# Two decoder blocks on one core: the first block's FFN up-projection with 512-column products and a PSUM bank per output tile

## The chip, the cores and the metric

The kernel runs on one core of a Trainium2 chip. It is one launch: weights and inputs come from device memory, a 256x1024 result goes back. The metric is the device time of that core in microseconds (us). TensorE is PE below, VectorE is DVE, ScalarE is ACT, GpSimdE is POOL.

## What is computed

Two blocks with two layers each. Every layer ends with an FFN. The FFN of the first block is the part that the change touches. With 256 tokens, model width 1024 and hidden width 2816:

```python
def causal_dwconv(x, w):              # K = 3 taps along the tokens
    y = xp[:, 0:S] * w[0]
    for j in range(1, K):
        y = y + xp[:, j:j + S] * w[j]

def conv_ffn(xn, w_up, conv_w, w_down):
    h = causal_dwconv(xn @ w_up, conv_w)      # 1024 -> 5632
    g, u = jnp.split(h, 2, axis=-1)
    return (jax.nn.silu(g) * u) @ w_down      # 2816 -> 1024

# first block, layer in (0, 1):
h = h + conv_ffn(rmsnorm(h, norm_ffn[layer]), ffn_w_up[layer], ffn_conv[layer], ffn_w_down[layer])
# second block: the same without the convolution
x = x + ((jax.nn.silu(a) * b) @ w_ffn_out[i])
```

## The kernel before

All large products are computed in three parts. A weight w and an activation x are each split into a high part (rounded to the fp32r format) and a low part (the remainder), and the product is w_hi·x_hi + w_hi·x_lo + w_lo·x_hi, accumulated in PSUM.

**Units and pieces.** Weights arrive as units of 1024x512 in a ring of two slots. A unit of the up-projection, `{L}up{j}` with j = 0 to 10, holds 256 gate columns and 256 up columns, so four output tiles of 128 channels x 256 tokens: tiles 0 and 1 are gate, 2 and 3 are up. A unit is eight pieces of 128x512. For each piece ACT writes `w_hi` (a copy that rounds, `round_weights`), POOL writes `w_lo` (ring minus `w_hi`, `remainders`), and PE multiplies. `w_hi` and `w_lo` have four places (HELD = 4). ACT may round piece p once PE has started piece p−3 (semaphore `piece_started`).

**PE in an up unit.** In block 1 (`split_channel_major`, lines 755 to 786) a piece is four times two products of 256 columns with `w_hi` (lines 774 and 777) and then four of 256 columns with `w_lo` (line 781). Two tiles share a 512-column bank; a unit uses two of banks 0 to 3. In block 2 the units up1 to up10 are WIDE (`split_wide`): x_hi and x_lo lie side by side in `x_pair`, so a piece is four products of 512 columns with `w_hi` (line 796) and four of 256 with `w_lo` (line 801). Each tile then has a bank of its own, with w_hi·x_lo in its second half.

**ACT and DVE in block 1 (`ffn_conv`, one on each engine).** For each pair q of tiles (q = 0 gate, q = 1 up), DVE multiplies the bank by the rows' norm factor R_b (`scale_bank`, line 2419, semaphore `ff_scaled`); ACT writes the last tap of the convolution into SBUF, two activations (`last_tap`, `ff_in`); DVE adds the two earlier taps with four instructions (`earlier_taps`, line 2456). After q = 0 a tiny copy on DVE (line 2461, `ff_conv`) releases ACT's SiLU (line 1845), which writes bank 4 or 5. DVE waits for it (`ff_act`), forms the product in bank 6 or 7 (line 2473), rounds it into `f_hi` and subtracts for `f_lo` (lines 2437 and 2439).

**Order.** Each engine follows its own program strictly in the written order; nothing is scheduled at run time. ACT, for unit j of block 1 with j > 0: last_tap(j,0), round pieces 0 and 1 of unit j+1, SiLU(j), round 2 and 3, last_tap(j,1), round 4 to 7. For j = 10 the following unit is down0, and only piece 2 is rounded between SiLU and last_tap(10,1). In layer 1 ACT also issues DMAs after the rounding (`load_block2`). DVE: scale(j,0), taps(j,0), scale(j,1), taps(j,1), product, split. The down projection follows with pieces of 128x512 rows; its piece 0 takes two banks (2 and 3), its piece 4 the other two (0 and 1).

Of the kernel before, what the change touches and what calls it, by code (L numbers as in the profile page):

```python
# [25 lines left out]
ALU = mybir.AluOpType  # L26
ACT = mybir.ActivationFunctionType
# [3 lines left out]
SEQ = 256  # L31
# [174 lines left out]
def build(nc, I, consts, out):  # L206

    ctx = ExitStack()
    with ctx:
# [203 lines left out]
        xs_ready = sem("xs_ready")  # L413
        ff_scaled = sem("ff_scaled")
        vec_ready = sem("vec_ready")
        zero_ready = sem("zero_ready")
# [134 lines left out]
        SPLIT = BY_CHANNELS | BY_TOKENS | BY_ROWS  # L551
        WIDE = {f"{L}up{j}" for L in (2, 3) for j in range(1, FF_UNITS)}
        AFTER_NORM = {"eq", "odq"} | {f"{L}up0" for L in range(4)} | {"2qr0", "3qr0"}
# [80 lines left out]
        def gains(key):  # L634

            L = int(key[0])
            if key == "2m":
                return lambda k: g_both[:, k:k + 1]
            name = {"m": "norm_mix", "x": "norm_xattn", "f": "norm_ffn"}[key[1]] + ("_g_2" if L >= 2 else "")
            r0 = ROWS[name][0] + 8 * (L % 2)  # L640
            return lambda k: vecs[:, r0 + k:r0 + k + 1]

        def turned_bank(key, k):
# [1005 lines left out]
        def _(act):  # L1649
# [175 lines left out]
            def ffn_conv(L):  # L1825
                first_unit(f"{L}up0", f"{L}f")
                r0 = ROWS["ffn_conv"][0] + L * 3 * 2 * FF_TILES + 2 * 2 * FF_TILES

                def last_tap(j, q):

                    n = L * FF_UNITS + j
                    key = (f"{L}up{j}", q)
                    b = B.uses[key][0]
                    act.wait_ge(ff_scaled, 2 * n + q + 1)
                    if q == 0 and n >= 2:
                        act.wait_ge(ff_h, n - 1)
                    for c in range(2):
                        row = r0 + q * FF_TILES + 2 * j + c
                        m = copy(f_y[j % 2][:, 2 * q + c, :], bank[b][:, c * SEQ:(c + 1) * SEQ], scale=vecs[:, row:row + 1])
# [292 lines left out]
        def _(dve):  # L2132
# [281 lines left out]
            def scale_bank(key):  # L2414
# [18 lines left out]

            def split_hidden(v, hi, lo, j):

                drain()
                nc.vector.tensor_copy(hi[:, 2 * j:2 * j + 2, :], v)
                drain()
                tt(lo[:, 2 * j:2 * j + 2, :], v, hi[:, 2 * j:2 * j + 2, :], ALU.subtract).then_inc(ff_h, 1)

            def ffn_conv(L):
# [4 lines left out]
                def earlier_taps(j, q):  # L2446

                    b, y = B.uses[(f"{L}up{j}", q)][0], f_y[j % 2]
                    dve.wait_ge(ff_in, 2 * (L * FF_UNITS + j) + q + 1)
                    for tap in (1, 0):  # L2450
# [3 lines left out]
                        for c in range(2):  # L2454
                            row = r0 + tap * 2 * FF_TILES + q * FF_TILES + 2 * j + c
                            m = stt(y[:, 2 * q + c, late:], bank[b][:, c * SEQ:(c + 1) * SEQ - late], vecs[:, row:row + 1],
                                    y[:, 2 * q + c, late:], ALU.mult, ALU.add)
                    m.then_inc(empty[b], 1)
                    drain()
# [3 lines left out]
                for j in range(FF_UNITS):  # L2463
                    scale_bank((f"{L}up{j}", 0))
                    if j == 0:
                        scale_bank((f"{L}up{j}", 1))
                    earlier_taps(j, 0)
                    if j:
                        scale_bank((f"{L}up{j}", 1))
                    earlier_taps(j, 1)  # L2470
                    dve.wait_ge(ff_act, L * FF_UNITS + j + 1)
                    product = bank[6 + j % 2][:, :]
                    tt(product, bank[4 + j % 2][:, :], f_y[j % 2][:, 2:4, :].rearrange("p a b -> p (a b)"), ALU.mult)
                    split_hidden(product.rearrange("p (a b) -> p a b", a=2), f_hi, f_lo, j)

# [446 lines left out]
```

## Time and profile before

| | |
|---|---|
| time, median of 3 runs | 2060.34 us (2060.13 to 2060.78) |
| the profiled execution, its own time | 2063.64 us |
| its span, first to last instruction | 2061.8 us |
| PE busy | 2014.0 us, 98% |
| POOL busy | 1624.4 us, 79% |
| ACT busy | 1088.3 us, 53% |
| DVE busy | 870.2 us, 42% |
| mean granted PE clock | 0.99 of full |

The span is what the trace covers; the time is 1.8 us more in the same execution, and the median of the unprofiled runs is 3.3 us under that. The up stage of layer 0 in block 1 lies at about 232 to 347 us of the span, that of layer 1 at about 713 to 828 us; the WIDE units of block 2 lie at about 1299 to 1411 us and 1881 to 1992 us. PE's ends are modelled, so the distance between starts of consecutive instructions says more than their durations.

### The profile page before, as it was taken

The numbers are of one execution on the slowest core, as the hardware profiler recorded it, in microseconds if no ns is written. First come the engines' busy times: TensorE is split into PE (matmuls) and PEld (weight loads), VectorE is DVE, ScalarE is ACT, GpSimd is POOL, SyncE is SP. The second block draws the span as 40 slices with busy tenths as digits, with TensorE's granted clock in tenths as the row PEclk, the third lists the DMA queues.
The fourth block names the chain that finished last, engine by engine and source line by source line (L and its number), as shares of the span: only waits on it lengthen the run. The fifth ranks groups of instructions, "written<-read, shape, count | busy, mean of one in ns | idle before, by whom it ended". The sixth has DMA issues, their size and how long they took to land.

```text
span 2061.8 us, 32417 instructions
## 1 busy us (share of the span) xinstructions
PE 2014.0 (98%) x12407; PEld 1755.8 (85%) x12407; DVE 870.2 (42%) x2029; ACT 1088.3 (53%) x2124; POOL 1624.4 (79%) x1293
## 2 busy tenths in 40 slices
PE   9999999999999999999999989999999999999998
PEld 8798999897889899898778858888997788678886
DVE  5512565065532466173323272563332412644551
ACT  4454665455244566445454585544444554865444
POOL 6595898976386798999799608899997897268998
PEclk9999999989999999999999999999999999999999
DMA  9753555543054476565446605555554466235553
GB/s 306 140 189 118 184 184 185 183 159 103 1 173 155 153 237 215 169 199 190 137 167 191 220 22 164 184 184 187 181 188 159 143 196 224 78 110 177 190 201 109
DMA packets 244271, 343.14 MB, mean 166 GB/s; under 512 B 8819, under 2 KB 172755, under 8 KB 243989
## 3 DMA queue, kind: packets, MB, share of 16 engines
q1 hardware_dynamic: 231832, 330.83, 48.7%
q10 hardware_dynamic: 12285, 10.24, 2.5%
q8 instruction: 99, 1.62, 0.3%
q14 instruction: 55, 0.45, 0.1%
HBM read 336.85 MB, written 4.19 MB: 165 GB/s over the span
## 4 chain that ended last, share of the span: by engine, by line
PE 84%; POOL 6%; DVE 3%; issue 3%; ACT 2%; POOLq 1%; DMA 1%; DVEq 0%; SPq 0%; ACTq 0%
PE bank L774 9%; PE bank L781 9%; PE bank L777 9%; PE bank L796 7%; PE bank L824 7%; PE bank L830 7%; PE bank L827 6%; POOL w_lo L1557 5%; PE bank L854 5%; PE bank L857 5%; PE bank L861 5%; PE bank L801 4%; DVE E L2271 1%; DVE E L2285 1%; PE bank L742 1%
## 5 line engine op out<-in xcount | busy, mean ns | idle before, releaser
L1557 POOL TENSOR_TENSOR w_lo<-ring,w_hi 128x512 fp32r<-128x512 f32 (+1 forms) x1216 | 1577.5, 1317 | 387.4 <-ACT w_hi L1652 351.3
L1652 ACT ACTIVATE w_hi<-ring 128x512 fp32r<-128x512 f32 (+1 forms) x1216 | 757.5, 630 | 789.2 <-PE bank L824 265.2
L774 PE MATMUL bank<-x_pair,w_hi 128*128 128x256 f32 x1504 | 380.8, 285 | 2.2 <-DVE x_pair L2171 1.5
L777 PE MATMUL bank<-x_pair,w_hi 128*128 128x256 f32 x1504 | 378.3, 284 | 0.0
L824 PE MATMUL bank<-w_hi,x_pair 128*128 128x512 f32 (+1 forms) x752 | 299.1, 398 | 2.6 <-issue 1.6
L774 PEld LDWEIGHTS bank<-x_pair,w_hi 128*128 128x128 f32 x1504 | 289.5, 192 | 5.0 <-issue 1.5
L827 PE MATMUL bank<-w_hi,x_pair 128*128 128x512 f32 (+1 forms) x752 | 292.8, 390 | 0.0
L777 PEld LDWEIGHTS bank<-x_pair,w_hi 128*128 128x128 f32 x1504 | 289.6, 193 | 0.4
L781 PE MATMUL bank<-x_pair,w_lo 128*128 128x256 f32 x1504 | 242.2, 283 | 0.0
L830 PE MATMUL bank<-w_lo,x_pair 128*128 128x512 f32 (+1 forms) x752 | 234.3, 393 | 3.4 <-POOL w_lo L1557 2.6
L781 PEld LDWEIGHTS bank<-x_pair,w_lo 128*128 128x128 f32 x1504 | 208.1, 193 | 0.0
L854 PE MATMUL bank<-w_hi,hidden 128*128 128x512 f32 x480 | 187.2, 390 | 0.0
L857 PE MATMUL bank<-w_hi,hidden 128*128 128x512 f32 x480 | 186.8, 389 | 0.0
L830 PEld LDWEIGHTS bank<-w_lo,x_pair 128*128 128x128 f32 x752 | 139.9, 190 | 41.3 <-POOL w_lo L1557 13.6
L796 PE MATMUL bank<-x_pair,w_hi 128*128 128x512 f32 x640 | 174.7, 394 | 0.0
L824 PEld LDWEIGHTS bank<-w_hi,x_pair 128*128 128x128 f32 x752 | 143.7, 191 | 33.1 <-issue 5.3
L827 PEld LDWEIGHTS bank<-w_hi,x_pair 128*128 128x128 f32 x752 | 143.7, 191 | 28.0 <-issue 0.7
L861 PE MATMUL bank<-w_lo,hidden 128*128 128x512 f32 x480 | 147.8, 389 | 0.0
L796 PEld LDWEIGHTS bank<-x_pair,w_hi 128*128 128x128 f32 x640 | 109.4, 189 | 14.7
L801 PEld LDWEIGHTS bank<-x_pair,w_lo 128*128 128x128 f32 x640 | 98.2, 189 | 13.6
L2163 DVE TENSOR_TENSOR h<-bank,h 128x512 f32<-128x512 f32 x36 | 23.1, 684 | 202.9 <-PE bank L861 153.7
L854 PEld LDWEIGHTS bank<-w_hi,hidden 128*128 128x128 f32 x480 | 90.1, 188 | 18.9 <-issue 0.4
(328 smaller groups left out, 2444.5 us busy)
## 6 DMA issues: line engine op xcount, KB each, us to landing
ring<-in_w_in SPq DMA_DIRECT2D x74, 1024.0 KB, 5.0
ring<-in_ffn_w_up SPq DMA_DIRECT2D x44, 1024.0 KB, 5.1
ring<-in_w_ffn_in SPq DMA_DIRECT2D x44, 1024.0 KB, 5.1
ring<-in_ffn_w_down SPq DMA_DIRECT2D x20, 1024.0 KB, 4.9
ring<-in_w_ffn_out SPq DMA_DIRECT2D x20, 1024.0 KB, 4.9
ring<-in_xattn_wkv SPq DMA_DIRECT2D x16, 1024.0 KB, 5.3
ring<-in_w_o_ret SPq DMA_DIRECT2D x16, 1024.0 KB, 4.9
ring<-in_od_w_in SPq DMA_DIRECT2D x12, 1024.0 KB, 5.2
```

Of the source, the lines that this page charges most:

```text
L774: m = mm(out_, view(w_hi)[:, k, :], x_hi[:, 4 * kh + k, :], start=start, stop=False)
L777: mm(out_, view(w_hi)[:, k, :], x_lo[:, 4 * kh + k, :], start=False, stop=False)
L781: m = mm(out_, view(w_lo)[:, k, :], x_hi[:, 4 * kh + k, :], start=False, stop=stop)
L796: m = mm(bank[b][:, :], view(w_hi)[:, k, :], x_pair[:, 4 * kh + k, :, :].rearrange("p a n -> p (a n)"), start=kh == 0 and k == 0, stop=False)
L824: m = mm(acc, hi, view(w_hi), start=k == 0, stop=False)
L827: mm(acc, lo, view(w_hi), start=False, stop=False)
L830: m = mm(bank[b0 + t][:, 0:n], x_hi[:, k, t * P:(t + 1) * P], view(w_lo), start=False, stop=k == KT - 1)
L854: m = mm(bank[b][:, :], hi, view(w_hi), start=kt == 0, stop=False)
L857: mm(bank[b][:, :], lo, view(w_hi), start=False, stop=False)
L861: m = mm(bank[b][:, :], x_hi[:, kt, t * P:(t + 1) * P], view(w_lo), start=False, stop=kt == tiles - 1)
L1557: tt(view(w_lo), src, view(w_hi), ALU.subtract).then_inc(w_lo_ready, 1)
L1652: return A(o, i_, ACT.Copy, **kw)
```

## The change

Units up1 to up10 of the two layers of block 1 become WIDE as well (unit up0 stays as it was). What follows from that in the code:

- PE: four 512-column products per piece in place of eight of 256 columns; a bank for each of the four tiles (0, 4, 1, 5 or 2, 6, 3, 7).
- ACT: `cross_terms(j, q)` copies the second half of two banks (w_hi·x_lo of two tiles) to the SBUF tile E, ahead of `last_tap(j, q)`.
- DVE: `scale_tiles` adds E to the first half of the bank, and multiplies by R_b, tile by tile.
- SiLU is written to the bank of the unit's first tile, and product and split happen there. A further tiny copy on DVE, after the split, releases that bank; the other three are released by the taps.

```diff
-        WIDE = {f"{L}up{j}" for L in (2, 3) for j in range(1, FF_UNITS)}
+        WIDE = {f"{L}up{j}" for L in range(4) for j in range(1, FF_UNITS)}
...
+                def cross_terms(j, q):
+
+                    if j == 0:
+                        return
+                    n = L * FF_UNITS + j
+                    if q == 0:
+                        act.wait_ge(ff_scaled, 2 * n)
+                    for c in (2 * q, 2 * q + 1):
+                        key = (f"{L}up{j}", c)
+                        B.wait_full(act, key)
+                        copy(E[:, c, 0:SEQ], bank[B.uses[key][0]][:, SEQ:2 * SEQ]).then_inc(ff_cross, 1)
...
-                    A(bank[4 + j % 2][:, :], f_y[j % 2][:, 0:2, :].rearrange("p a b -> p (a b)"), ACT.Silu).then_inc(ff_act, 1)
+                    A(bank[B.uses[f"{L}up{j}", 0][0]][:, :], f_y[j % 2][:, 0:2, :].rearrange("p a b -> p (a b)"), ACT.Silu).then_inc(ff_act, 1)
...
                     else:
+                        cross_terms(j, 0)
                         last_tap(j, 0)
                         round_weights(following, 0, 2)
                         silu(j)
                         round_weights(following, 2, HELD - 1 if j + 1 == FF_UNITS else HELD)
+                        cross_terms(j, 1)
                         last_tap(j, 1)
...
+            def scale_tiles(L, j, q):
+
+                if j == 0:
+                    return scale_bank((f"{L}up{j}", q))
+                for c in range(2):
+                    dve.wait_ge(ff_cross, 4 * (L * (FF_UNITS - 1) + j - 1) + 2 * q + c + 1)
+                    v = up_tile(L, j, q, c)
+                    tt(v, v, E[:, 2 * q + c, 0:SEQ], ALU.add)
+                drain()
+                for c in range(2):
+                    v = up_tile(L, j, q, c)
+                    m = tt(v, v, R_b[:, :], ALU.mult)
+                m.then_inc(ff_scaled, 1)
...
                 tt(lo[:, 2 * j:2 * j + 2, :], v, hi[:, 2 * j:2 * j + 2, :], ALU.subtract).then_inc(ff_h, 1)
+                drain()
+                nc.vector.tensor_copy(small[:, 22, 1:2], small[:, 23, 1:2]).then_inc(empty[b], 1)
```

Three places show what stands where. ACT in unit j = 3 of layer 0, before: two last-tap activations (`region<-bank2`), two roundings, SiLU (line 1845), two roundings, the other pair.

```order
L1652 ACTIVATE region<-bank2,vecs 128x256 [waits ff_h,ff_scaled]
L1652 ACTIVATE region<-bank2,vecs 128x256
L1652 ACTIVATE w_hi<-ring 128x512 [waits piece_started,half0_landed0]
L1652 ACTIVATE w_hi<-ring 128x512 [waits piece_started]
L1845 ACTIVATE bank6<-region 128x512 [waits ff_conv]
```

ACT in the same unit after the change, up to the roundings of pieces 4 to 7.

```order
L1660 ACTIVATE E<-bank2 128x256 [waits bank_full2,ff_scaled]
L1660 ACTIVATE E<-bank6 128x256 [waits bank_full6]
L1660 ACTIVATE region<-bank2,vecs 128x256 [waits ff_h,ff_scaled]
L1660 ACTIVATE region<-bank6,vecs 128x256
L1660 ACTIVATE w_hi<-ring 128x512 [waits piece_started,half0_landed0]
L1660 ACTIVATE w_hi<-ring 128x512 [waits piece_started]
L1863 ACTIVATE bank2<-region 128x512 [waits ff_conv]
L1660 ACTIVATE w_hi<-ring 128x512 [waits piece_started,half0_landed0]
L1660 ACTIVATE w_hi<-ring 128x512 [waits piece_started]
L1660 ACTIVATE E<-bank3 128x256 [waits bank_full3]
L1660 ACTIVATE E<-bank7 128x256 [waits bank_full7]
L1660 ACTIVATE region<-bank3,vecs 128x256 [waits ff_scaled]
```

Two copies to E stand ahead of each pair of last taps; those of the second pair (banks 3 and 7) stand behind the SiLU and two roundings.

DVE from the product of the unit before (line 2473) to the taps of this one, before.

```order
L2473 TENSOR_TENSOR bank6<-bank4,region 128x512 [waits ff_act]
L2437 CAST hidden<-bank6 128x512
L2439 TENSOR_TENSOR hidden<-bank6,hidden 128x512
L2419 TENSOR_TENSOR bank2<-bank2,R_b 128x512 [waits bank_full2]
L2456 SCALAR_TENSOR_TENSOR region<-bank2,vecs,region 128x255 [waits ff_in]
```

The same stretch of DVE after the change, and on to the second pair of tiles.

```order
L2513 TENSOR_TENSOR bank0<-bank0,region 128x512 [waits ff_act]
L2472 CAST hidden<-bank0 128x512
L2474 TENSOR_TENSOR hidden<-bank0,hidden 128x512
L2476 COPY small<-small 128x1
L2448 TENSOR_TENSOR bank2<-bank2,E 128x256 [waits ff_cross]
L2448 TENSOR_TENSOR bank6<-bank6,E 128x256 [waits ff_cross]
L2452 TENSOR_TENSOR bank2<-bank2,R_b 128x256
L2452 TENSOR_TENSOR bank6<-bank6,R_b 128x256
L2493 SCALAR_TENSOR_TENSOR region<-bank2,vecs,region 128x255 [waits ff_in]
```

One multiplication of 512 columns has become two additions and two multiplications of 256, and the additions wait for ACT's copies where the multiplication waited for PE.

PE at the fifth piece of down0 (k = 0 of its second half of columns), after the change; before, the row reads the same with line 854.

```order
L862 MATMUL bank0<-w_hi,hidden 128x512 [waits w_hi_ready,bank_empty1,bank_empty0]
L865 MATMUL bank0<-w_hi,hidden 128x512
```

What moved there is not the row but what empties bank 0: before, the taps of pair 0 of unit up10 (line 2456); now the tiny copy behind the split of that unit (line 2476).

## Rows read from the trace of the kernel before

**Rows 1.** The page: PE's busy time, share and instructions.
```profile
PE 2014.0 (98%) x12407; PEld 1755.8 (85%) x12407; DVE 870.2 (42%) x2029; ACT 1088.3 (53%) x2124; POOL 1624.4 (79%) x1293
```

**Rows 2.** Windows, busy us of each engine (instructions), clock, DMA share, GB/s.
```profile
core 0: us, PE busy (x) PEld busy (x) DVE busy (x) ACT busy (x) POOL busy (x), PEclk, DMA share, GB/s
242.50:333.50 91.00, 91.00 (x761) 91.00 (x760) 57.55 (x114) 57.66 (x104) 83.04 (x65) 1.00 0.58 186
1310.00:1411.00 101.00, 101.00 (x578) 88.25 (x578) 60.51 (x176) 50.36 (x90) 93.83 (x73) 1.00 0.57 187
```

**Rows 3.** Lines, 242 to 335 us: busy, mean ns, idle before, releaser.
```profile
L774 PE MATMUL bank<-x_pair,w_hi 128*128 128x256 f32 x259 | 65.0, 283 | 0.0
L1652 ACT ACTIVATE w_hi<-ring 128x512 fp32r<-128x512 f32 x66 | 41.6, 632 | 31.1 <-PE bank L774 30.4
```

**Rows 4.** Timeline (start, us, instruction): PE, consecutive pieces in block 1 and block 2.
```profile
269.52 0.28 PE L774 MATMUL bank<-x_pair,w_hi 128*128 128x256 f32 x1
...
270.96 0.28 PE L774 MATMUL bank<-x_pair,w_hi 128*128 128x256 f32 x1
...
1324.35 1.09 PE L796 MATMUL bank<-x_pair,w_hi 128*128 128x512 f32 x4
...
1325.75 1.09 PE L796 MATMUL bank<-x_pair,w_hi 128*128 128x512 f32 x4
```

**Rows 5.** Timeline of ACT in unit up10 of layer 0: last taps, then SiLU.
```profile
342.45 0.84 ACT L1652 ACTIVATE region<-bank,vecs 128x256 f32<-128x256 f32 x2
...
345.43 0.60 ACT L1845 ACTIVATE bank<-region 128x512 f32<-128x512 f32 x1
```

**Rows 6.** Timeline of ACT in unit up1 of layer 0.
```profile
240.56 0.84 ACT L1652 ACTIVATE region<-bank,vecs 128x256 f32<-128x256 f32 x2 [1.77 <-DVE bank L2419]
...
243.53 0.60 ACT L1845 ACTIVATE bank<-region 128x512 f32<-128x512 f32 x1 [1.09 <-DVE small L2461]
244.07 1.14 ACT L1652 ACTIVATE w_hi<-ring 128x512 fp32r<-128x512 f32 x2
245.11 0.82 ACT L1652 ACTIVATE region<-bank,vecs 128x256 f32<-128x256 f32 x2
```

**Rows 7.** ACT: block 2's SiLU of two tiles (timeline); copies to E (by lines).
```profile
1328.12 0.64 ACT L2109 ACTIVATE region<-bank 128x256 f32<-128x256 f32 x2
...
L1652 ACT ACTIVATE E<-bank 128x256 f32<-128x256 f32 x4 | 1.5, 380 | 5.4 <-PE bank L1371 5.3
```

**Rows 8.** Timeline of DVE, 256-column operations and the tiny copy in block 2.
```profile
1320.62 0.42 DVE L2427 TENSOR_TENSOR bank<-bank,R_b 128x256 f32<-128x256 f32 x1
...
1321.78 0.76 DVE L2431 TENSOR_TENSOR bank<-bank,E 128x256 f32<-128x256 f32 x2
...
1330.60 0.76 DVE L2866 TENSOR_TENSOR hidden<-bank,hidden 128x256 fp32r<-128x256 f32 x2
...
1331.52 0.41 DVE L2426 TENSOR_TENSOR E<-bank,R_b 128x256 f32<-128x256 f32 x1
```

**Rows 9.** Timeline of DVE in layer 0: taps, product, and last step of the split.
```profile
326.05 1.82 DVE L2456 SCALAR_TENSOR_TENSOR region<-bank,vecs,region 128x255 f32<-128x255 f32 x4 [0.91 <-ACT region L1652]
327.96 0.70 DVE L2473 TENSOR_TENSOR bank<-bank,region 128x512 f32<-128x512 f32 x1
...
329.50 0.69 DVE L2439 TENSOR_TENSOR hidden<-bank,hidden 128x512 fp32r<-128x512 f32 x1
```

**Rows 10.** Timeline: DVE's split of unit up0, and PE's down0 piece 4, layer 0.
```profile
239.23 0.69 DVE L2439 TENSOR_TENSOR hidden<-bank,hidden 128x512 fp32r<-128x512 f32 x1
...
352.75 0.39 PE L854 MATMUL bank<-w_hi,hidden 128*128 128x512 f32 x1
```

**Rows 11.** Timeline, layer 1: ACT at unit up1, and DVE's taps of pair 0 of up10.
```profile
719.05 2.57 ACTq L1876 DMA_DIRECT2D region<-constants  x5
721.74 0.84 ACT L1652 ACTIVATE region<-bank,vecs 128x256 f32<-128x256 f32 x2 [2.44 <-DVE bank L2419]
...
823.84 1.82 DVE L2456 SCALAR_TENSOR_TENSOR region<-bank,vecs,region 128x255 f32<-128x255 f32 x4 [0.91 <-ACT region L1652]
```

**Rows 12.** Windows, columns as in Rows 2: a stretch in which PE is idle a fifth.
```profile
550.00:560.00 10.00, 7.85 (x63) 7.28 (x64) 7.04 (x18) 1.28 (x8) 1.21 (x2) 1.00 0.00 0
```

More of the change, by code:

```diff
@@ L414, in build @@
         ff_scaled = sem("ff_scaled")
+        ff_cross = sem("ff_cross")
         vec_ready = sem("vec_ready")
@@ L641, in gains, with up_tile @@
             return lambda k: vecs[:, r0 + k:r0 + k + 1]
+        def up_tile(L, j, q, c):
+            name = f"{L}up{j}"
+            if name in WIDE:
+                return bank[B.uses[name, 2 * q + c][0]][:, 0:SEQ]
+            return bank[B.uses[name, q][0]][:, c * SEQ:(c + 1) * SEQ]
         def turned_bank(key, k):
@@ L1827, in ffn_conv @@
                 r0 = ROWS["ffn_conv"][0] + L * 3 * 2 * FF_TILES + 2 * 2 * FF_TILES
+                def cross_terms(j, q):
[8 more added lines that the diff above has]
+                        copy(E[:, c, 0:SEQ], bank[B.uses[key][0]][:, SEQ:2 * SEQ]).then_inc(ff_cross, 1)
                 def last_tap(j, q):
                     n = L * FF_UNITS + j
-                    key = (f"{L}up{j}", q)
-                    b = B.uses[key][0]
                     act.wait_ge(ff_scaled, 2 * n + q + 1)
@@ L1838, in last_tap @@
                         row = r0 + q * FF_TILES + 2 * j + c
-                        m = copy(f_y[j % 2][:, 2 * q + c, :], bank[b][:, c * SEQ:(c + 1) * SEQ], scale=vecs[:, row:row + 1])
+                        m = copy(f_y[j % 2][:, 2 * q + c, :], up_tile(L, j, q, c), scale=vecs[:, row:row + 1])
                     m.then_inc(ff_in, 1)
@@ L2432, in scale_wide, with split_hidden @@
                 m.then_inc(ff_scaled, 1)
-            def split_hidden(v, hi, lo, j):
+            def split_hidden(b, hi, lo, j):
+                v = bank[b][:, :].rearrange("p (a b) -> p a b", a=2)
                 drain()
@@ L2446, in earlier_taps @@
                 def earlier_taps(j, q):
-                    b, y = B.uses[(f"{L}up{j}", q)][0], f_y[j % 2]
+                    name, y = f"{L}up{j}", f_y[j % 2]
                     dve.wait_ge(ff_in, 2 * (L * FF_UNITS + j) + q + 1)
@@ L2455, in earlier_taps @@
                             row = r0 + tap * 2 * FF_TILES + q * FF_TILES + 2 * j + c
-                            m = stt(y[:, 2 * q + c, late:], bank[b][:, c * SEQ:(c + 1) * SEQ - late], vecs[:, row:row + 1],
+                            m = stt(y[:, 2 * q + c, late:], up_tile(L, j, q, c)[:, 0:SEQ - late], vecs[:, row:row + 1],
                                     y[:, 2 * q + c, late:], ALU.mult, ALU.add)
-                    m.then_inc(empty[b], 1)
+                            if tap == 0 and j and (q or c):
+                                m.then_inc(empty[B.uses[name, 2 * q + c][0]], 1)
+                            if tap == 0 and j == 0 and q and c:
+                                m.then_inc(empty[B.uses[name, q][0]], 1)
                     drain()
@@ L2463, in ffn_conv @@
                 for j in range(FF_UNITS):
-                    scale_bank((f"{L}up{j}", 0))
+                    scale_tiles(L, j, 0)
                     if j == 0:
-                        scale_bank((f"{L}up{j}", 1))
+                        scale_tiles(L, j, 1)
                     earlier_taps(j, 0)
                     if j:
-                        scale_bank((f"{L}up{j}", 1))
+                        scale_tiles(L, j, 1)
                     earlier_taps(j, 1)
                     dve.wait_ge(ff_act, L * FF_UNITS + j + 1)
-                    product = bank[6 + j % 2][:, :]
-                    tt(product, bank[4 + j % 2][:, :], f_y[j % 2][:, 2:4, :].rearrange("p a b -> p (a b)"), ALU.mult)
-                    split_hidden(product.rearrange("p (a b) -> p a b", a=2), f_hi, f_lo, j)
+                    b = B.uses[f"{L}up{j}", 0][0]
+                    tt(bank[b][:, :], bank[b][:, :], f_y[j % 2][:, 2:4, :].rearrange("p a b -> p (a b)"), ALU.mult)
+                    split_hidden(b, f_hi, f_lo, j)
             cross(0)
```

## The prediction

> **What bounds the kernel now.** Read the busy shares first [rows 1]: PE is busy 98% of the span, so a stage costs what PE costs in it, as long as the other engines keep up. The table by stage [rows 2] shows that in both up stages PE never pauses, while POOL works 83 of 91 us, ACT 58 and DVE 58. The groups by line [rows 3] say the same from the other side: PE's products have no idle time before them, and ACT's roundings spent 31.1 us waiting, 30.4 of it for PE. So in block 1 ACT and DVE are followers with slack, and the stage goes at PE's pace. The timeline gives that pace [rows 4]: a piece starts 1.44 us after the last one in block 1 (269.52 to 270.96) and 1.40 us in the WIDE units of block 2 (1324.35 to 1325.75). A unit of eight pieces is 11.52 us against 11.22 us.
>
> **What the change buys on PE.** 0.037 us a piece (11.22/8 against 1.44), 8 pieces, 10 units, 2 layers: 5.9 us, if PE goes on setting the pace. Rows stand for this: block 2 does the same products. The Trainium skill has a rule that speaks against even that (TensorE: Matmul & The Clock Gate, section "Wait — 56ns, not 53.3ns?"): a warm matmul starts N/2.4 GHz plus about 2.5 ns after the one before. By that page a piece would be estimated at 12 x 109 ns = 1.31 us before and 4 x 216 + 4 x 109 = 1.30 us after, a gain of 1.6 us in all. The rows differ from it, with 120 ns for each 256-column product (1.44/12), and they decide.
>
> **What the change adds.** PE needs rounded weights, and these come from ACT, which does its list in order. So the question is how long ACT and DVE need for one unit when each waits for the other. I follow one unit round the loop, from T0, the end of the two last-tap activations of pair 0, to the same point one unit later. Each step starts when the one before has ended:
>
> 1. T0 to the start of SiLU (DVE's taps of pair 0 and the tiny copy lie in between): 342.45+0.84 = 343.29 to 345.43, 2.14 us [rows 5]. The two roundings that ACT does meanwhile are hidden.
> 2. SiLU and two roundings, start of SiLU to start of the next activation: 243.53 to 245.11, 1.58 us [rows 6].
> 3. Two copies to E, which is the added wait: DVE can do nothing for pair 1 before. Plain copies of this form have a row of 380 ns for one [rows 7]; for two in a row the nearest is the SiLU of two tiles, 0.64 us. Bounds: 0.64 and 2 x 0.38 = 0.76. I take 0.64, since activations overlap in all rows of pairs, plus 0.04 to reach DVE: 0.68.
> 4. The second addition (0.42), a drain (0.07) and two multiplications (0.76) [rows 8]: 1.25. The drain is what is left between 0.70 busy and the 0.77 from step to step of product and split, half of 327.96 to 329.50 [rows 9].
> 5. ACT's two last taps of pair 1, as DVE's idle time shows it: 0.91 [rows 9].
> 6. DVE's taps of pair 1 to the start of the product: 326.05 to 327.96, 1.91.
> 7. Product and split: 327.96 to 329.50+0.69, 2.23.
> 8. The new tiny copy that frees the bank: 1330.60+0.76 to 1331.52, 0.16 [rows 8].
> 9. Two additions, drain, two multiplications for pair 0 of the next unit: 0.76+0.07+0.76 = 1.59. Their copies to E are ready by then: ACT is through with the last taps of pair 1 at T0+6.5, with four roundings of 0.52 each (244.07 to 245.11 is two) at about 8.5 and with the copies at about 9.2, against 10.9.
> 10. ACT's last taps of pair 0: 0.87 (0.91 less the way to DVE).
>
> The sum is 13.32 us. That is more than PE's 11.22 and more than the 11.52 of now, so **this loop takes over as the bound**. Before the change the loop did not close this way: DVE scaled pair 1 as soon as PE had it, without ACT. Now pair 1 waits behind SiLU and two roundings, and SiLU waits for DVE. What queues behind ACT's waits is rounding, so POOL's remainders and PE's pieces come late: PE waits some 2.1 us a unit, before pieces 0 and 4, on `w_hi`. POOL needs 8 x 1.28 (83.04/65 [rows 2]) = 10.2 us of each 13.3 and stays out of it.
>
> ACT standing still at a wait while later work is ready is in the rows: 1.09 us before SiLU at 243.53 [rows 6]. The Trainium skill states it as a rule (PSUM — Partial Sum Buffer, section "Engine vs sequencer instructions"): the ScalarE and VectorE queues are strictly first in, first out.
>
> **Layer 0.** Unit up1: DVE's split of up0 ends at 239.23+0.69 = 239.92 [rows 10]; plus steps 8 to 10 (0.16+1.59+0.87) T0 is 242.54, where it was 240.56+0.84 = 241.40 [rows 6]. Nine loops of 13.32 are 119.9, so T0 of up10 comes at 362.4 instead of 343.3 [rows 5]: +19.1. Then a second cost: piece 4 of down0 takes bank 0, which now is free only after up10's split. From T0 that is steps 1 to 7 with one rounding fewer (10.70−0.52) and about 0.2 for the copy, 10.4; before, piece 4 started at 352.75 [rows 10], 9.46 after T0. That adds 0.9 to 1.0. Behind it the down stage runs at PE's pace as before, so the loss stays: 20.1 us.
>
> **Layer 1.** ACT issues DMAs ahead of up1 until 719.05+2.57 = 721.62 and then did the last taps at 721.74 [rows 11]. Now the copies start there: 721.74+0.64+0.04+1.25+0.87 = 724.54 against 722.58, +1.96. T0 of up10: 724.54+119.9 = 844.4 against 823.8, +20.6; with the bank 21.6 us. The DMA issues of the later units (two each) fall where ACT has 1.7 us of slack.
>
> Sum 41.7 us. The profiled execution took 2063.64 (span 2061.8); the median is 3.3 lower, and I add to the median: 2060.3+41.7 = **2102.0 us**, 2.0% slower. A measurement of this kernel can tell about 0.2% (4 us) from no change.
>
> **Rivals.**
> *The clock falls.* PE would be idle 2.1 of 13.3 us, in pieces of about 1 us. Where it was idle 2.15 of 10 us, the granted clock stayed at 1.00 [rows 12], the 2.4 GHz level. If it fell to 1.2 GHz, a unit would need 22.4 us of PE, more than the loop; ten such units among the twenty would add (22.4−13.3) x 10 = 91 us at most, two of them 18: about 2120.
> *DVE alone sets the pace.* If the copies of pair 1 were always there in time, the loop would be steps 1, 9, 5, 6, 7, 8, 9 and 10: 2.14+1.59+0.91+1.91+2.23+0.16+1.59+0.87 = 11.40, near the 11.52 of now. T0 of up10 would be late by 1.8 and 3.4 us (1.14 and 1.96 at the start, and 9 x 11.40 = 102.6 against 101.9 and 101.2), less 0.4 in each layer since bank 0 is free at 9.0 and not at 9.46: 2064.6. For it: each engine alone has time enough. Against it: the written order, SiLU ahead of these copies.
> *The other side, faster.* If the loop took less than 11.22, PE's pace held and the 5.9 us came: 2054.4. It decides at 11.22: the loop would have to be 2.1 us shorter than my sum, and no single step but the first, sixth and seventh is as much as that. The page's matmul rule would make of this 2058.7.
>
> **Chances.** Forecast 0.87; clock 0.06; DVE alone 0.04; faster 0.03. Within the forecast an error of 0.35 us in the loop is 18 x 0.35 = 6.3 us, and step 3 at its upper bound adds 0.12 x 18 = 2.2; something of the steps may also overlap more than single rows show, so I go further down than up: 2090 to 2112. That leaves out the rivals (0.13) and a little of the forecast. Slower by over 0.2%: 0.87, 0.06 and half of DVE alone, 0.95; within 0.2%: 0.02; faster: 0.03.
>
> **What would show it.** Right: in a middle unit of layer 0 the taps of pair 0 start 13.3 us apart; DVE's first addition for pair 1 waits about 2.0 us for ACT's copy (step 2 and the first copy of step 3); PE idles before `w_hi` of two pieces a unit; block 2's up stages are unchanged at 11.22; down0's piece 4 waits for DVE's tiny copy. Wrong: a distance of 11.2 (PE) or 11.4 (DVE alone); a granted clock under 1.00 in the stage; additions from E much longer than 0.42, or PE waits for POOL.

## The result and the profile after

| | before | after |
|---|---|---|
| time, median of 4 runs each | 2060.24 us (2057.85 to 2060.78) | 2108.18 us (2106.6 to 2112.93) |
| the profiled execution | 2063.64 us, span 2061.8 | 2106.6 us, span 2104.8 |
| ratio | | 1.024 (95%: 1.0224 to 1.0257) |

The change makes the kernel 2.4% slower. The forecast was 2102.0 in a range of 2090 to 2112.

**The page.** The busy shares, to be laid beside [rows 1]:

```profile
PE 2027.7 (96%) x11767; PEld 1717.1 (82%) x11767; DVE 901.8 (43%) x2171; ACT 1097.6 (52%) x2204; POOL 1621.3 (77%) x1293
```

PE has 640 instructions fewer and a share of 96% instead of 98. POOL and ACT have a smaller share than before, and DVE has one point more, 43% instead of 42: nothing here names a bound.

**The windows.** An up stage of block 1 in layer 0, then the two in block 2 (columns as in Rows 2):

```profile
262.00:355.00 93.00, 84.39 (x445) 67.23 (x444) 61.51 (x147) 52.25 (x118) 70.40 (x56) 1.00 0.48 159
...
1353.00:1454.00 101.00, 101.00 (x577) 88.26 (x576) 60.54 (x175) 50.36 (x90) 93.62 (x74) 1.00 0.58 187
1935.00:2035.00 100.00, 100.00 (x572) 87.40 (x571) 59.60 (x173) 49.80 (x89) 92.72 (x73) 1.00 0.57 185
```

In [rows 2] PE filled its 91 us. Now it is busy 84 of 93, at a granted clock of 1.00, while block 2 is as full as it was. By line, in the same stretch:

```profile
L804 PE MATMUL bank<-x_pair,w_hi 128*128 128x512 f32 x221 | 61.3, 398 | 6.9 <-ACT w_hi L1660 6.9
```

In [rows 3] the products waited for nothing; now they wait for ACT's rounding. But look at what ACT itself waits for (waits, 245 to 360 us: total, times, longest):

```profile
ACT region L1660 <- DVE bank L2452: 39.6, 17, 3.7
POOL w_lo L1565 <- ACT w_hi L1660: 27.8, 26, 2.1
DVE bank L2448 <- ACT E L1660: 18.1, 9, 2.0
DVE region L2493 <- ACT region L1660: 15.4, 17, 0.9
...
PEld bank L809 <- POOL w_lo L1565: 9.4, 17, 0.6
ACT bank L1863 <- DVE small L2501: 8.8, 8, 1.1
```

ACT waits for DVE and DVE for ACT, in turn. That is a loop of two engines, with neither of them full: in the window above DVE is busy 61.5 of 93 us and ACT 52.3. The rows of POOL and of PEld (PE's loading of weights) show how the lateness travels: POOL waits for ACT's `w_hi`, and PE then waits for POOL's `w_lo`, 0.6 us at most each time. One unit of it on DVE's timeline:

```profile
255.63 1.82 DVE L2493 SCALAR_TENSOR_TENSOR region<-bank,vecs,region 128x255 f32<-128x255 f32 x4 [0.91 <-ACT region L1660]
257.54 0.15 DVE L2501 COPY small<-small 128x1 f32<-128x1 f32 x1
259.70 0.76 DVE L2448 TENSOR_TENSOR bank<-bank,E 128x256 f32<-128x256 f32 x2 [2.01 <-ACT E L1660]
260.54 0.77 DVE L2452 TENSOR_TENSOR bank<-bank,R_b 128x256 f32<-128x256 f32 x2
262.21 1.82 DVE L2493 SCALAR_TENSOR_TENSOR region<-bank,vecs,region 128x255 f32<-128x255 f32 x4 [0.91 <-ACT region L1660]
264.13 0.70 DVE L2513 TENSOR_TENSOR bank<-bank,region 128x512 f32<-128x512 f32 x1
...
265.66 0.69 DVE L2474 TENSOR_TENSOR hidden<-bank,hidden 128x512 fp32r<-128x512 f32 x1
266.45 0.15 DVE L2476 COPY small<-small 128x1 f32<-128x1 f32 x1
266.52 0.75 DVE L2448 TENSOR_TENSOR bank<-bank,E 128x256 f32<-128x256 f32 x2
```

And the same on ACT's:

```profile
254.75 0.84 ACT L1660 ACTIVATE region<-bank,vecs 128x256 f32<-128x256 f32 x2 [3.34 <-DVE bank L2452]
...
257.73 0.60 ACT L1863 ACTIVATE bank<-region 128x512 f32<-128x512 f32 x1 [1.09 <-DVE small L2501]
258.26 1.14 ACT L1660 ACTIVATE w_hi<-ring 128x512 fp32r<-128x512 f32 x2
259.30 0.64 ACT L1660 ACTIVATE E<-bank 128x256 f32<-128x256 f32 x2
...
268.14 0.84 ACT L1660 ACTIVATE region<-bank,vecs 128x256 f32<-128x256 f32 x2 [3.34 <-DVE bank L2452]
```

From one last tap of pair 0 to the next ACT takes 268.14−254.75 = 13.39 us. Read the third DVE line first: 2.01 us of idle time, and the copies that it waits for start at 259.30, the moment at which ACT is through with SiLU and two roundings.

**Where the 43.0 us of span went.** DVE writes R_b anew at every norm (around layer 0's FFN at 230.85 and 421.50 us before, at 230.42 and 444.15 us after). Between those marks the distance of before and after can be compared stage by stage:

| stretch from norm to norm | before | after | difference |
|---|---|---|---|
| FFN of block 1, layer 0 | 190.65 | 213.73 | +23.1 |
| the stage behind it | 214.02 | 209.36 | −4.7 |
| FFN of layer 1 | 230.10 | 252.69 | +22.6 |
| all else, to the end | 1427.0 | 1429.0 | +2.0 |

Both FFNs took the loss that was expected of them. The −4.7 is most likely not the change's: no instruction differs there, and the windows (columns as above) of before and of after show another granted clock, 0.90 and 0.95.

```profile
421.00:521.00 100.00, 96.97 (x594) 87.85 (x593) 58.57 (x122) 57.03 (x100) 67.27 (x53) 0.90 0.35 116
```

```profile
444.00:544.00 100.00, 96.97 (x635) 87.79 (x634) 60.56 (x125) 58.79 (x104) 69.43 (x54) 0.95 0.35 115
```

The profiled execution of before is 3.4 us over its median, that of after 1.6 under: 43.0+3.4+1.6 = 48.0, the 47.9 between the medians.

### The profile page after: what moved, and what is told of

It reads as the page before. It is cut to its first block, busy times and chain, and to the rows that moved or that the text cites. A ratio compares the mean times of both kernels' runs of the same rounds, so it can differ in the third digit from the quotient of the medians.

```text
span 2104.8 us, 31481 instructions
## 1 busy us (share of the span) xinstructions
PE 2027.7 (96%) x11767; PEld 1717.1 (82%) x11767; DVE 901.8 (43%) x2171; ACT 1097.6 (52%) x2204; POOL 1621.3 (77%) x1293
## 4 chain that ended last, share of the span: by engine, by line
PE 70%; DVE 10%; POOL 6%; ACT 5%; issue 5%; DVEq 3%; DMA 1%; POOLq 1%; ACTq 0%; SPq 0%
PE bank L804 7%; PE bank L832 7%; PE bank L838 7%; PE bank L835 6%; PE bank L782 5%; PE bank L789 5%; POOL w_lo L1565 5%; PE bank L785 5%; PE bank L862 5%; PE bank L865 5%; PE bank L869 5%; PE bank L809 4%; DVE region L2493 2%; ACT w_hi L1660 2%; DVE bank L2452 1%
## 5 line engine op out<-in xcount | busy, mean ns | idle before, releaser
L1660 ACT ACTIVATE w_hi<-ring 128x512 fp32r<-128x512 f32 (+1 forms) x1216 | 747.1, 629 | 727.0 <-PE bank L832 266.5
L804 PE MATMUL bank<-x_pair,w_hi 128*128 128x512 f32 x1280 | 351.7, 396 | 17.4 <-ACT w_hi L1660 17.4
L804 PEld LDWEIGHTS bank<-x_pair,w_hi 128*128 128x128 f32 x1280 | 218.3, 189 | 52.6 <-issue 23.5
L809 PEld LDWEIGHTS bank<-x_pair,w_lo 128*128 128x128 f32 x1280 | 192.8, 189 | 44.9 <-POOL w_lo L1565 20.1
L782 PE MATMUL bank<-x_pair,w_hi 128*128 128x256 f32 x864 | 219.0, 286 | 1.5 <-DVE x_pair L2191 0.7
L785 PE MATMUL bank<-x_pair,w_hi 128*128 128x256 f32 x864 | 216.5, 283 | 0.0
L809 PE MATMUL bank<-x_pair,w_lo 128*128 128x256 f32 x1280 | 207.3, 284 | 4.4
L838 PEld LDWEIGHTS bank<-w_lo,x_pair 128*128 128x128 f32 x752 | 140.4, 191 | 41.7 <-POOL w_lo L1565 14.3
L782 PEld LDWEIGHTS bank<-x_pair,w_hi 128*128 128x128 f32 x864 | 165.5, 192 | 4.2 <-issue 2.2
L785 PEld LDWEIGHTS bank<-x_pair,w_hi 128*128 128x128 f32 x864 | 165.6, 192 | 0.4
L789 PE MATMUL bank<-x_pair,w_lo 128*128 128x256 f32 x864 | 138.8, 283 | 0.0
L789 PEld LDWEIGHTS bank<-x_pair,w_lo 128*128 128x128 f32 x864 | 119.2, 192 | 0.0
```

Source lines behind the costliest of these rows:

```text
L782: m = mm(out_, view(w_hi)[:, k, :], x_hi[:, 4 * kh + k, :], start=start, stop=False)
L785: mm(out_, view(w_hi)[:, k, :], x_lo[:, 4 * kh + k, :], start=False, stop=False)
L789: m = mm(out_, view(w_lo)[:, k, :], x_hi[:, 4 * kh + k, :], start=False, stop=stop)
L804: m = mm(bank[b][:, :], view(w_hi)[:, k, :], x_pair[:, 4 * kh + k, :, :].rearrange("p a n -> p (a n)"), start=kh == 0 and k == 0, stop=False)
L809: m = mm(bank[b][:, 0:SEQ], view(w_lo)[:, k, :], x_hi[:, 4 * kh + k, :], start=False, stop=kh == 1 and k == 3)
L838: m = mm(bank[b0 + t][:, 0:n], x_hi[:, k, t * P:(t + 1) * P], view(w_lo), start=False, stop=k == KT - 1)
```

## The experiments

All are variants of the changed kernel, each timed against runs of the kernel before on the same chip; compare the ratios rather than the medians. "Loop" is the distance of DVE's taps of pair 0 from unit to unit in the middle of layer 0 (with one digit: of ACT's SiLUs).

| | median us | ratio to before (95%) | loop us |
|---|---|---|---|
| before | | 1 | 11.52 (PE's pace) |
| after | 2108.18 | 1.0240 (1.0224 to 1.0257) | 13.39 |
| one pair of roundings fewer ahead of the copies | 2089.18 | 1.0142 (1.0126 to 1.0157) | 12.36 |
| copies ahead of SiLU | 2066.01 | 1.0029 (1.0017 to 1.0041) | 11.34 |
| DVE takes both halves | 2092.33 | 1.0156 (1.0141 to 1.0171) | 12.60 |
| no second half | 2053.16 | 0.9969 (0.9957 to 0.9982) | 11.23 |
| other banks in the last unit | 2101.28 | 1.0196 (1.0182 to 1.0210) | 13.4 |
| product in the gap | 2066.30 | 1.0034 (1.0021 to 1.0047) | 11.23 |
| the same, edge of layer 1 mended | 2065.14 | 1.0028 (1.0017 to 1.0039) | 11.3 |
| the same, both edges mended | 2059.35 | 0.9999 (0.9990 to 1.0008) | 11.3 |
| and ACT's DMA issues moved | 2056.90 | 0.9984 (0.9975 to 0.9993) | 11.3 |

### Is it the place of the copies?

The theory: pair 1's copies to E stand behind SiLU and two roundings, and the loop is the sum of what the two engines do in turn. The first experiment moves one thing past another on ACT, the second one more.

```diff
                         silu(j)
-                        round_weights(following, 2, HELD - 1 if j + 1 == FF_UNITS else HELD)
                         cross_terms(j, 1)
+                        round_weights(following, 2, HELD - 1 if j + 1 == FF_UNITS else HELD)
```

> Changed kernel, with ACT's two copies of pair 1 moved ahead of the two roundings, directly behind SiLU. Theory 1 (the loop of waits between ACT and DVE runs through SiLU, two roundings and these copies): the loop loses the two roundings, 2 x 0.52 us, and goes from the 13.39 us of the changed kernel to 12.35; 18 loops and the last unit of each layer give about 20 us back, 2088 us. Theory 2 (it is the amount of work added to ACT that makes its roundings late, in whatever order): 13.4 us a unit and 2108. Theory 3 (DVE's own added work is the bound): 13.4 us a unit and 2108.

```diff
                         round_weights(following, 0, 2)
+                        cross_terms(j, 1)
                         silu(j)
                         round_weights(following, 2, HELD - 1 if j + 1 == FF_UNITS else HELD)
-                        cross_terms(j, 1)
```

> Changed kernel, with ACT's two copies of pair 1 moved ahead of SiLU as well. Theory 1: DVE no longer waits for SiLU, and what is left of the loop is DVE with two pairs of last taps, 2.14+1.59+0.91+1.91+2.23+0.16+1.59+0.87 = 11.40 us a unit; 18 x 1.99 and 1 to 2 us for the bank, so about 2070 us. DVE's first addition for pair 1 waits for nothing or little. Theories 2 and 3 (amount of work on ACT, or on DVE): still 13.4 us and 2108.

Measured: 2089.18 and 2066.01 us. The first additions for pair 1, on DVE, in the first experiment and then in the second:

```profile
293.35 1.82 DVE L2493 SCALAR_TENSOR_TENSOR region<-bank,vecs,region 128x255 f32<-128x255 f32 x4 [0.91 <-ACT region L1660]
...
296.39 0.76 DVE L2448 TENSOR_TENSOR bank<-bank,E 128x256 f32<-128x256 f32 x2 [0.97 <-ACT E L1660]
...
305.71 0.88 DVE L2493 SCALAR_TENSOR_TENSOR region<-bank,vecs,region 128x255 f32<-128x255 f32 x2 [0.91 <-ACT region L1660]
```

```profile
297.95 1.82 DVE L2493 SCALAR_TENSOR_TENSOR region<-bank,vecs,region 128x255 f32<-128x255 f32 x4 [0.91 <-ACT region L1660]
299.86 0.15 DVE L2501 COPY small<-small 128x1 f32<-128x1 f32 x1
299.93 0.75 DVE L2448 TENSOR_TENSOR bank<-bank,E 128x256 f32<-128x256 f32 x2
...
309.29 0.87 DVE L2493 SCALAR_TENSOR_TENSOR region<-bank,vecs,region 128x255 f32<-128x255 f32 x2 [0.91 <-ACT region L1660]
```

The wait goes from 2.01 to 0.97 to nothing, the loop from 13.39 to 12.36 to 11.34. Two roundings out of the chain are worth 1.03 us a unit, SiLU with the copies another 1.02. The second kernel has the loop of the rival "DVE alone" to 0.06 us (worked out as 11.40) and a time (2066.0) near the 2064.6 worked out for it. So the mechanism is shown, and so is what remains: with the order mended this way the 512-column form is in the middle of a stage only 0.18 us a unit under PE's old pace (11.52), and the whole is 0.3% slower. Its FFN stretches are 1.6 us (layer 0) and 6.0 us (layer 1) longer than before's. Part of layer 1's loss is inside the stage: two DMA issues of ACT in unit up2 took 2.39 us there, and that loop 12.55 us.

### Is it ACT's share or the added work?

Here DVE does it alone, as in block 2: no copies on ACT, each half multiplied by R_b and then added, so DVE's four instructions of 256 columns for a pair of tiles become six.

```diff
-                for c in range(2):
-                    dve.wait_ge(ff_cross, 4 * (L * (FF_UNITS - 1) + j - 1) + 2 * q + c + 1)
-                    v = up_tile(L, j, q, c)
-                    tt(v, v, E[:, 2 * q + c, 0:SEQ], ALU.add)
...
+                scale_wide(f"{L}up{j}", (2 * q, 2 * q + 1))
```

> ACT makes no copies; DVE scales both halves of each bank and adds them, as block 2 does (2.25 us a pair instead of 1.59, more work for DVE, none added on ACT). Theory 1: the wait for ACT's copies goes, DVE's longer pairs come: 2.14+2.25+0.91+1.91+2.23+0.16+2.25+0.87 = 12.72 us a unit, 2090 to 2095 us. Theory 2 (ACT's added work): the stage returns to PE's 11.2 us, 2055. Theory 3 (DVE's added work): 0.66 us more for each of 40 pairs, 2134.

Measured: 2092.33 us, loop 304.65−292.05 = 12.60. ACT's copies are gone, and it is still slow. The loop is 0.12 under the 12.72 worked out for it: DVE's longer chain, with its waits for ACT's last taps and SiLU, is over PE's pace. The handover costs less than DVE's extra instructions, if it stands in the right place (11.34).

The next leaves w_hi·x_lo of units up1 to up10 in block 1 out of the result: no copies on ACT and no additions on DVE. PE does the same work as in the changed kernel, 512 columns with `w_hi`, and the order and the banks are the same too; the second halves of the banks are just not read.

```diff
-                    tt(v, v, E[:, 2 * q + c, 0:SEQ], ALU.add)
...
+                    B.wait_full(dve, (f"{L}up{j}", 2 * q + c))
```

> The wide products, the banks and the place of SiLU stay, but ACT makes no copies and DVE no additions: the product of w_hi with the low part of x is left out of up1 to up10 in both layers of block 1. All theories of a loop expect it to fall to 2.14+0.76+0.91+1.91+2.23+0.16+0.76+0.87 = 9.74 us, under PE's 11.22: PE sets the pace, the distance between units is 11.22 and the time 2055 us, 5 to 6 under the kernel before. If banks, or SiLU in the first tile's bank, cost in every unit, it stays above 2060.

Measured: 2053.16 us, loop 11.23. Without the handover PE sets the pace again:

```profile
299.31 0.43 DVE L2446 TENSOR_TENSOR bank<-bank,R_b 128x256 f32<-128x256 f32 x1 [1.23 <-PE bank L809]
...
305.24 0.76 DVE L2446 TENSOR_TENSOR bank<-bank,R_b 128x256 f32<-128x256 f32 x2
```

```profile
262.00:325.00 63.00, 63.00 (x361) 55.08 (x360) 40.95 (x96) 40.16 (x76) 57.96 (x46) 1.00 0.57 185
```

DVE now waits for PE, not for ACT, and PE is full with all its wide products. The bank per tile, SiLU in the first tile's bank and the later release are all still in: none of them slows the middle of the stage.

### What does the bank at the end of the stage cost?

Piece 4 of down0 takes the banks that up10's first tile holds until its split is done. The edit lets up10 use its two sets of banks the other way round, so that piece 4 finds a free one.

```diff
+        LAST_UP = {f"{L}up{FF_UNITS - 1}" for L in range(2)}
...
-                    b = b0 + c // 2 + 4 * (c % 2)
+                    b = b0 + c // 2 + 4 * ((c + (name in LAST_UP)) % 2)
```

> Changed kernel, with the banks of a pair swapped in unit up10 alone: its first tile, where SiLU, product and split happen, lies in bank 4 and not in bank 0. Piece 4 of down0 then waits for the taps and for w_hi (about 8.0 us after T0 of up10) and not for the tiny copy behind the split (10.5 us). If that release was on the path: 2.4 us in each layer, 2103 us. If PE was held there by something else anyway: 2108.

Measured: 2101.28 us, 6.9 below the changed kernel (the ratios, 1.0240 and 1.0196, say 0.0044 or 9 us; each against its own runs of the kernel before). Totals of two kernels also hold what stages without an edit did, so take the FFN stretches of the traces: 209.98 instead of 213.73 us in layer 0 and 251.33 instead of 252.69 in layer 1. That is 5.1 us together, about the 4.8 expected, but not in equal parts. In layer 1, 0.7 of the missing microsecond went at the entry, which the edit does not touch: there the first SiLUs were 10.58 us apart instead of 9.86. PE's timeline of after, layer 0, shows what else was in that layer's loss:

```profile
369.71 0.50 PE L862 MATMUL bank<-w_hi,hidden 128*128 128x512 f32 x1 [1.19 <-ACT w_hi L1660]
...
373.62 0.50 PE L862 MATMUL bank<-w_hi,hidden 128*128 128x512 f32 x1 [1.80 <-DVE small L2476]
373.96 0.40 PE L865 MATMUL bank<-w_hi,hidden 128*128 128x512 f32 x1
...
375.64 0.63 PE L865 MATMUL bank<-w_hi,hidden 128*128 128x512 f32 x1
376.07 0.63 PE L862 MATMUL bank<-w_hi,hidden 128*128 128x512 f32 x1
...
378.75 0.39 PE L865 MATMUL bank<-w_hi,hidden 128*128 128x512 f32 x1
```

From 375.2 to 378.2 the products start 0.43 us apart instead of 0.23, and the granted clock of that window is 0.50. The windows of the same 10 us, of after and then of this experiment:

```profile
370.00:380.00 10.00, 8.03 (x27) 5.80 (x27) 3.16 (x7) 3.24 (x7) 8.13 (x7) 0.83 0.53 190
```

```profile
370.00:380.00 10.00, 9.82 (x43) 7.80 (x44) 3.31 (x7) 5.17 (x9) 10.00 (x9) 1.00 0.53 189
```

The granted clock fell behind the 1.80 us wait and not where the wait is gone: 10 x (1−0.83) = 1.7 us more. These are single executions, and after the same wait in layer 1 the clock did not fall (last section), so that the bank edit is what removed the dip is likely, but not shown.

### Can the chain be shortened below PE's pace?

SiLU's wait for DVE and DVE's wait for the copies can cover each other. DVE does product and split of unit j−1 while ACT works on pair 0 of unit j; ACT does both pairs' copies and taps before SiLU. This kernel includes the bank edit.

```diff
                         cross_terms(j, 0)
                         last_tap(j, 0)
                         round_weights(following, 0, 2)
-                        silu(j)
-                        round_weights(following, 2, HELD - 1 if j + 1 == FF_UNITS else HELD)
                         cross_terms(j, 1)
+                        round_weights(following, 2, HELD - 1 if j + 1 == FF_UNITS else HELD)
                         last_tap(j, 1)
+                        silu(j)
...
                 for j in range(FF_UNITS):
                     scale_tiles(L, j, 0)
+                    if j == 0:
+                        scale_tiles(L, j, 1)
+                    else:
+                        finish_unit(j - 1)
                     earlier_taps(j, 0)
...
+                finish_unit(FF_UNITS - 1)
```

(`finish_unit` is the wait for SiLU, the product and the split, as they stood at the end of the unit.)

> The copies of pair 1 ahead of everything that waits for DVE, SiLU behind the last taps of pair 1, the banks swapped in up10, and on DVE the product and split of a unit placed behind the scaling of pair 0 of the next unit, where DVE had stood 0.9 us waiting for ACT. All the work of the change is done. If the 11.4 us loop left over was DVE's work plus two waits for ACT, one wait hidden gives 10.5, less than PE's 11.22: PE sets the pace, and the time is 2054 to 2056 us, 4 to 6 under the kernel before. If something else holds the loop at 11.4: 2064 to 2066.

Measured: 2066.30 us, a miss by 10. The loop of layer 0 is as expected (303.58−292.35 = 11.23). In the middle of layer 1's stage PE's busy time looks full:

```profile
754.00:820.00 66.00, 66.00 (x366) 55.94 (x367) 50.17 (x122) 42.56 (x97) 58.38 (x47) 1.00 0.72 224
```

But the window has 366 of PE's products, where the last kernel of this section has 376 in the same 66 us, and its SiLUs are 11.61 to 11.64 us apart; this loss is taken up below. The other thing that the expectation left out were the edges. At the entry of layer 1, ACT (ACTq is its issuing of DMAs) and DVE:

```profile
716.39 3.05 ACTq L1897 DMA_DIRECT2D region<-constants  x5
719.56 0.66 ACT L1661 ACTIVATE E<-bank 128x256 f32<-128x256 f32 x2 [2.91 <-issue]
```

```profile
719.98 0.76 DVE L2449 TENSOR_TENSOR bank<-bank,E 128x256 f32<-128x256 f32 x2 [4.41 <-ACT E L1661]
...
721.49 0.69 DVE L2508 TENSOR_TENSOR bank<-bank,region 128x512 f32<-128x512 f32 x1
```

The product of up0 now stands behind these additions and so behind ACT's six DMA issues, and PE waits for the bank that it holds:

```profile
724.01 1.21 PE L805 MATMUL bank<-x_pair,w_hi 128*128 128x512 f32 x4 [2.65 <-DVE small L2477]
```

At the end of each layer piece 3 of down0 waits 0.8 to 0.9 us, because its rounding stands behind the last tap and SiLU. Two kernels mend this. In both, up0 finishes behind its own taps, and the six issues are spread over up1 to up3 (not among the lines shown, which are against the product-in-the-gap kernel); the second one also rounds pieces 2 and 3 of down0 together (shown against the first).

```diff
-                    else:
+                    elif j > 1:
                         finish_unit(j - 1)
...
+                    if j == 0:
+                        finish_unit(j)
```

> As the kernel beside it, but ACT rounds only piece 2 of down0 ahead of the last tap in unit up10, as in the product-in-the-gap kernel. PE waits again about 0.8 to 0.9 us for w_hi of piece 3 of down0 in each layer: 2057 to 2060 us, 1.5 to 2.5 above the kernel beside it.

```diff
-                        round_weights(following, 2, HELD - 1 if j + 1 == FF_UNITS else HELD)
+                        round_weights(following, 2, HELD)
                         last_tap(j, 1)
                         silu(j)
-                        round_weights(following, HELD - 1 if j + 1 == FF_UNITS else HELD)
+                        round_weights(following, HELD)
```

> The product-in-the-gap order again, with three edits at its edges: unit up0 keeps its product and split behind its own taps; in unit up10 ACT rounds pieces 2 and 3 of down0 together, ahead of the last tap; in layer 1 the six DMA issues of ACT at the end of unit up0 are spread over units up1 to up3. Theory: the loop was already at PE's pace (11.23 us), and what kept that kernel above the one before were the waits of PE at the edges, 2.8 us for the bank at the entry of layer 1 and about 0.9 us for w_hi of piece 3 of down0 in each layer, with what the chain loses behind them. Then PE waits nowhere in the up stages and the kernel comes to 2055 to 2058 us, faster than the one before by 0.1 to 0.3%. Rival: the 512-column form costs something in the stage besides waits, then it stays at 2062 or more with no idle time of PE at either edge.

Measured: 2065.14 and 2059.35. Both medians lie above what was expected. The edges did what was said of them: PE no longer waits at the entry, and between the two kernels the FFN stretches differ by 0.9 (layer 0) and 1.0 us (layer 1). The other 3.9 us between their medians are in stages that no edit touches, with other granted clocks, and are not explained. In the mended kernel PE's rows show almost no idle time in layer 1, and yet from up3 on a unit there takes 11.47 to 11.75 us between SiLUs, most of them 11.61 to 11.64, against 11.24 to 11.32 in layer 0. What only layer 1 has is this on ACT:

```profile
770.84 0.37 ACTq L1905 DMA_DIRECT2D region<-distance_table  x1
...
771.24 0.53 ACTq L1905 DMA_DIRECT2D region<-distance_table  x1
771.87 0.66 ACT L1661 ACTIVATE E<-bank 128x256 f32<-128x256 f32 x2 [0.27 <-issue]
```

The last kernel moves all 18 of ACT's DMA issues of layer 1 to units down1 to down5.

```diff
+                parts = [-6, -5, -4, -3, -2, -1] + list(range(1, BIAS_LOADS + 1)) if L == 1 else []
                 for j in range(1, DOWN_UNITS):
-                    round_weights(f"{L}down{j}")
+                    for p in range(0, pieces(f"{L}down{j}"), 2):
+                        round_weights(f"{L}down{j}", p, p + 2)
+                        if parts:
+                            load_block2(parts.pop(0))
```

> The kernel with all edges mended, and ACT's 18 DMA issues of layer 1 (for block 2's constants and bias) moved out of the up stage: one behind every second rounding of units down1 to down5, where ACT waits some 0.7 us for PE at every piece. In that kernel the distance of ACT's SiLUs in layer 0 was 11.24 to 11.32 us and in layer 1 11.61 to 11.64, with two such issues a unit (about 0.4 to 0.5 us each). Theory: the issues stretch the loop of layer 1 past PE's pace, and without them it is 11.3 there too: 8 x 0.35 = 2.8 us less, 2056 to 2057, ahead of the kernel before by 0.15%. Rival: the distance in layer 1 stays at 11.6, and then it is something else in that layer (POOL, or the weights' DMAs), and the time stays at 2059.

Measured: 2056.90 us against 2061.22 of before on the same chip, ratio 0.9984 (0.9975 to 0.9993). The SiLUs of layer 1 are from up2 on 11.22 to 11.32 us apart, two of them at

```profile
778.68 0.60 ACT L1864 ACTIVATE bank<-region 128x512 f32<-128x512 f32 x1
...
789.96 0.60 ACT L1864 ACTIVATE bank<-region 128x512 f32<-128x512 f32 x1
```

and the rival (something else in that layer) has fallen. Layer 1's FFN stretch is 3.0 us shorter than in the kernel with both edges mended (228.70 against 231.69), where 2.8 were expected. This is the one version, with all of the computation in it, that is ahead of both kernels. In its trace the FFN stretches are 1.15 (189.50 against 190.65) and 1.4 us (228.70 against 230.10) shorter than before's, 2.6 together. The rest of the 4.3 us between the medians lies elsewhere: the stage behind layer 0's FFN ran at a clock of 0.97 in this trace and 0.90 in before's, and the runs don't say whether that belongs to the kernel.

## Why the prediction was right

**The loop.** 13.32 was worked out, 13.39 measured, and every step has its row. With T0 = 254.75+0.84 = 255.59:

| step | predicted | measured |
|---|---|---|
| 1, T0 to SiLU | 2.14 | 2.14 (to 257.73) |
| 2, SiLU and two roundings | 1.58 | 1.57 (to 259.30) |
| 3 and 4, copies, additions, multiplications | 1.93 | 2.01 (to 261.31) |
| 5, last taps of pair 1 | 0.91 | 0.90 (to 262.21) |
| 6, DVE's taps | 1.91 | 1.92 (to 264.13) |
| 7, product and split | 2.23 | 2.22 (to 266.35) |
| 8, tiny copy | 0.16 | 0.17 (to 266.52) |
| 9, pair 0 scaled | 1.59 | 1.59 (to 268.11) |
| 10, last taps of pair 0 | 0.87 | 0.87 (to 268.98) |

The one step that was not in the trace of before, the handover, came with step 4 to 0.08 more than the value taken, inside the bounds of step 3 (0.12). Eighteen loops of 0.07 are 1.3 us.

**The sum.** Layer 0: entry +1.2 (predicted 1.14), nine loops +19.0 (18.0; one of them took 13.76), bank 10.54 after T0 instead of 10.4, which is +1.1 (0.9 to 1.0): 21.3 against 20.1. Layer 1: entry +2.1 (1.96), nine loops +19.3 (18.7), bank +1.1: 22.5 against 21.6. Together 43.8 against 41.7.

**What the sum lacked** is the dip of the clock behind the wait for the bank, 1.7 us in layer 0, and it is a term that the sum had at nothing: the step "behind it the down stage runs at PE's pace as before" was wrong there. The sum had only the 1.0 by which piece 4 comes later, not a wait of 1.80 us with a clock that can fall behind it. With the dip the FFN stretches are at 45.5, as measured 45.7. What is left up to the 47.9 between the medians lies in stages that the change does not touch and in the spread of single executions (3.4 and 1.6 us, above). So the range held with 3.8 us to spare at its upper end, and the steps of the loop, not the closeness of the total, are the evidence for the mechanism.

**The points of "what would show it".** Taps 13.3 apart: 13.39. The first addition waits about 2.0: 2.01. PE idle before two pieces a unit: yes. It loses 13.39−11.23 = 2.16 us a unit. PE's rows have 0.58 and 0.35 us of idle time before the `w_hi` products of two pieces (at 256.26 and 262.84), and the loading of the `w_lo` weights of the same pieces waits another 0.56 us each time, for POOL (9.4 us in 17 waits, above). One of the signs of being wrong, "PE waits for POOL", thus did come. It does not name another bound: POOL was busy 70.4 of 93 us and had itself waited for ACT's `w_hi`, 27.8 us in 26 waits. In the kernel without the second half POOL does the same work, and there (262 to 325 us) PE waited for it nowhere. Block 2 unchanged: yes. Piece 4 waits for the tiny copy: yes. The granted clock stayed at 1.00 in the up stage.

**The rivals.** *The clock falls* did not come in the stage it was put in; the clock fell behind its end, for 3 us. *DVE alone* was not what happened, but it is what the kernel with the copies ahead of SiLU does, to 0.06 us in the loop. *Faster* needed a loop under 11.22. The prediction held this to be out of reach because only its first, sixth and seventh step are as much as 2.1 us (the sixth, 1.91, is not). The product-in-the-gap order got to PE's pace (11.23 to 11.33 in layer 0) without removing a step, by letting two waits cover each other. With the edges mended and the issues moved, the gain was 2.6 us of the 5.9.

**The pages.** The wide piece started 1.40 us apart (264.70 to 266.10 on PE), as in block 2; the Trainium skill (TensorE: Matmul & The Clock Gate, section "Wait — 56ns, not 53.3ns?") would give an estimate of 1.30, and the measurement decides. The Trainium skill also states that the ScalarE and VectorE queues are strictly first in, first out (PSUM — Partial Sum Buffer, section "Engine vs sequencer instructions"). The first two experiments agree: the same copies, moved past two roundings and SiLU, are worth 1.03 and 1.02 us a unit.

## What to carry to other kernels

When a change adds a handover between two engines that already take turns, write down the ring of one iteration (who waits for whom, in the written order) and add it up. The busy shares say nothing about it: here the only engine that was fuller afterwards, DVE, went from 42% to 43%, and the loop went from hidden to 1.9 us over the old pace. Put what the other engine waits for ahead of everything on which nobody waits, and let independent work (a product of the iteration before) fill the turn. Then look at the first and last iteration and at DMA issues on a computing engine's queue, which here together cost more than the middle had gained: 1.0034 of the time before with them, 0.9984 without.

## What the hardware showed that was not expected

The clock fell behind short waits. Up to the end of the up stage PE lost 2.2 us of every 13.4 to waits, at two places, and kept a granted clock of 1.00. Behind the 1.8 us wait for the bank (1.78 to 1.81 us in all cases) it ran some 3 us at the lower of its two levels (1.2 GHz; granted clock 0.50, starts 0.43 us apart instead of 0.23), in after in layer 0 but not in layer 1. In the four kernels that have this wait it stands in eight places, and the clock fell behind five of them; in the kernel with other banks, which differs in nothing else, the wait and the dip are gone in both layers. What decides between the five and the three is open, and each kernel was traced in one execution.

How the granted clock falls in stages that no edit touches differed from trace to trace: in the stage behind layer 0's FFN it was 0.90 (before), 0.95 (after) and 0.97 (the last kernel) over 100 us, with the same instructions there. From norm to norm the stage took 214.02, 209.36 and 207.82 us: up to 6 us, as much as the whole gain that was at stake. For a change worth 0.2%, compare the stretch that it edits, and only then the total.

A wait shows only in part in PE's rows: 0.58 and 0.35 us of idle time stood there for 2.16 us lost. Another 0.56 us for each of the two pieces stood in the rows of the weight loads, where PE waited for `w_lo`. The distance of starts from unit to unit gave the whole.
